# Scaling attention weights before mixing, or mixed values after it: a change in two of four attentions of a two-block transformer kernel

## The chip, the cores and the metric

The kernel runs on one core of one Trainium2 chip. The metric is the device time of one execution in microseconds. The core's engines are TensorE (PE, with its weight loads as PEld), VectorE (DVE), ScalarE (ACT), GpSimd (POOL) and SyncE (SP), which issues most DMAs. Each engine works through its own instructions in order; semaphores tie them together.

## The reference

Two diffusion-transformer blocks run one after the other on 256 latent and 256 context tokens of width 1024, in fp32. The first has feed-forward layers and two mixers, the second two mixers. Each mixer projects, runs an attention beside a recurrent or linear branch, and projects back. What matters here is the attention of the first block's mixers:

```python
# even mixer: 8 query heads, 2 key heads of width 64
def attend(q, k, v):
    s = jnp.einsum('bqhgd,bkhd->bhgqk', q, k).astype(jnp.float32)
    p = jax.nn.softmax(s, axis=-1).astype(v.dtype)
    return jnp.einsum('bhgqk,bkhd->bqhgd', p, v)
# odd mixer: 16 query heads, 4 key heads; window of 128 positions, context keys, and a sink
s_win = jnp.where(valid, s_win, NEG_BIG)
p = softmax_with_sink(jnp.concatenate([s_win, s_ctx], axis=-1))
o = p[..., :span] @ vb + p[..., span:] @ v_c
```

The softmax's division by the row's sum can stand before the product with the values or behind it. The second block has an MLA attention with an mLSTM branch, and a neighbourhood attention with a gated linear one.

## The kernel before

All activations lie transposed in SBUF: a tile has 128 channels on its partitions and 512 tokens along them (`T`; the latent ones are columns `TC` = 256 to 512). Weights stream through a ring in slabs of 128x1024. ScalarE rounds each slab to its high part (L422), VectorE subtracts to get the low part (L427, `split_lo`), and TensorE multiplies high by high, high by low and low by high (L530 to L532; L538 to L541 where both halves stand in one tile).

**An attention** goes over pairs: two heads (a channel tile `t`) and 128 query tokens (`qt`). `attention_pairs` lists 16 pairs for "even", of which 8 see two key tiles and 8 see four, and 16 for "odd", which see three each. The functions `attend_tensor`, `attend_vector` and `attend_scalar` are generators that walk the same iterations `it`, a software pipeline over pairs:

- TensorE: scores of pair `it` (L1538); transposes of the weights of pair `it-2` (L1553), into banks 4 and 5; product with the values of pair `it-3` (L1571), into a bank from `mix_bank`.
- VectorE: `find_max` of pair `it` (for "odd" a mask is added first, L1595; the maximum is L1601, for "odd" followed by small sink terms, L1605 and L1607); `scale_weights` of pair `it-1` (for "odd" the sums are put together, L1616 and L1619; reciprocal L1622 of two sums a token, drain, two scalings of the weights, L1626, then the semaphore `probs_scaled`); for "even" the copy of the mixed values of pair `it-4` (L1641).
- ScalarE: for "odd" the copy of the mixed values of pair `it-4` (L1654, L1657 rounds a finished tile); copy of the transposed weights of pair `it-2` to SBUF (L1664); two exponentials of pair `it` with their sums (L1679).

TensorE may start the transposes of a pair when `probs_scaled` has counted it. Between these steps `keep_streaming` (L469) puts matmuls of ones with no use for their result, 128 columns each, at places from the table `STREAMED_BEFORE_TURNS`. A matmul of fp32 data has two records in the trace.

**Even attention** stands alone between the even projection and the chunked recurrence ("wkv"). Beside its iterations VectorE does some rotary sums (L1772 to L1781) and the decay sums of the recurrence (L2704, L2710, after two of the iterations), ScalarE three decay exponentials (L2556 to L2558), and GpSimd prepares the recurrence's keys (L2637 to L2647). The recurrence starts when the last mixed values are copied (`mixed_copied`).

**Odd attention** runs beside the odd input projection: for each of eight query slabs TensorE does a slab's 24 matmuls, turns the queries for the rotary sum (L1818), and takes two iterations of the attention. VectorE rotates the queries (L1842 to L1848) and splits the next slab. At its end stand the first two slabs of the output projection: `odd_out_half` is called for slab 0 ahead of the last mixing and for slab 1 behind it. `residual_vector` splits both slabs and six, then two more, tiles of the mixer's output (L1245) for them.

**The mLSTM branch** of the second block has 8 units (head and direction). `mlstm_tensor` makes scores for a head (L3125) and sums for each unit (L3140), which wait for `unit_done` of the unit before and for its own weights. `mlstm_vector` weighs unit `u` (L3040), normalises unit `u-1` (L3052 to L3065, with a reciprocal of four numbers, L3057) and masks unit `u+2` (L3030). Ahead of the sums of units 0 and 2 stand ten matmuls of ones.

Of the kernel before, what the change touches and what calls it, by code (L numbers as in the profile page):

```python
# [23 lines left out]
ALU = mybir.AluOpType  # L24
# [3 lines left out]
P = 128  # L28
D = 1024
KT = D // P  # L30
TC = 256
# [229 lines left out]
def build(nc, xin, ctx2, condrows, stream_k, stream_f, vecs, consts, tables, small, nabias, out):  # L261
# [4 lines left out]
    with ExitStack() as ctx:  # L266
# [122 lines left out]
        probs_ready = sem("probs_ready")  # L389
        probs_scaled = sem("probs_scaled")  # L390
        probs_turned = sem("probs_transposed")
# [78 lines left out]

        STREAMED_BEFORE_TURNS = {("even", 0): 4, ("even", 1): 3, ("even", 6): 11, ("odd", 10): 8, ("odd", 14): 7}
        STREAMED_BEFORE_ODD_SLAB = {5: (0, 7), 7: (6, 6)}
# [774 lines left out]
        def residual_vector(dve, r):  # L1247
# [3 lines left out]
            if r == 1:  # L1251
                split_lo(dve, first_place(stage, 0), n0, s0 + 1)
                for kt in range(6):
                    odd_tile_lo(dve, kt)
                split_lo(dve, 1, n0 + 1, s0 + 2)
                for kt in range(6, KT):
                    odd_tile_lo(dve, kt)
# [235 lines left out]
        def attention_turned(which, u):  # L1493

            two = BIG[:, 16 + u % 2 * 2:18 + u % 2 * 2, :] if which == "odd" else WORK[:, 20 + u % 2 * 2:22 + u % 2 * 2, :]
            return two.rearrange("p b t -> p (b t)")

        def mix_bank(which, u):

            return pb[6] if which == "odd" else pb[6 + u % 2]  # L1500

        def attend_tensor(pe, a):
# [12 lines left out]
            for it in range(n + 3):  # L1515
# [25 lines left out]
                if 0 <= u < n:  # L1541
# [4 lines left out]
                    keep_streaming(pe, pb[4], STREAMED_BEFORE_TURNS.get((which, u), 0))  # L1546
                    pe.wait_ge(probs_scaled, u0 + u + 1)
                    nt = len(key_tiles(which, pairs[u][1]))
                    for b in range(2):
                        for i in range(nt):  # L1550
                            o = slice((b * nt + i) * HD, (b * nt + i + 1) * HD)
                            for h, half in enumerate(HALF):
                                mm = pe.transpose(pb[4 + h][:, o], attention_probs(which, u)[half, b, tok(i)], C("ident")[half, half])  # L1553
                    mm.then_inc(probs_turned, 1)
                u = it - 3
                if 0 <= u < n:
# [18 lines left out]
                    if which == "odd" and u == n - 1:  # L1575
                        odd_out_half(pe, 1, range(KT - 1))
                yield

        def attend_vector(dve, a):
# [30 lines left out]
            def scale_weights(u):  # L1610
# [4 lines left out]
                if which == "odd":  # L1615
                    dve.tensor_tensor(st[:, 4, :], st[:, 4, :], st[:, 3, :], ALU.add)  # L1616
                    dve.drain()
                    if pairs[u][1] == 3:
                        dve.scalar_tensor_tensor(out=st[:, 4, :], in0=st[:, 2, :], scalar=C("padkeys"), in1=st[:, 4, :],  # L1619
                                                 op0=ALU.mult, op1=ALU.add)  # L1620
                        dve.drain()
                dve.reciprocal(st[:, 1, :], st[:, 4, :])  # L1622
                dve.drain()
                for b in range(2):
                    probs = attention_probs(which, u)[:, b, 0:nk]
                    ins = dve.tensor_scalar(probs, probs, st[:, 1, b:b + 1], None, ALU.mult)  # L1626
                ins.then_inc(probs_scaled, 1)

            for it in range(n + 4):
                turns_first = which == "odd" and it in (1, 13)  # L1630
                if turns_first:
# [5 lines left out]
                u = it - 4  # L1637
                if 0 <= u < n and which != "odd":
                    t, qt = pairs[u]
# [5 lines left out]
        def attend_scalar(act, a):  # L1645
# [3 lines left out]
            for it in range(n + 4):  # L1649
                u = it - 4  # L1650
                if 0 <= u < n and which == "odd":
                    t, qt = pairs[u]
                    act.wait_ge(mixed, u0 + u + 1)
                    act.activation(BIG[:, t, qt * P:qt * P + P], pb[6][:, 0:P], ACT.Copy).then_inc(mixed_copied, 1)  # L1654
                    if qt == 3:
                        act.drain()
                        act.activation(out_hi(1, t), BIG[:, t, TC:T], ACT.Copy).then_inc(mixer_hi, 1)  # L1657
                u = it - 2
                if 0 <= u < n:
                    nk = len(key_tiles(which, pairs[u][1])) * P  # L1660
                    act.wait_ge(probs_turned, u0 + u + 1)
                    if u >= 2:
                        act.wait_ge(mixed, u0 + u - 1)
                    act.activation(crossed(attention_turned(which, u)[:, 0:2 * nk]),  # L1664
# [1453 lines left out]
        def mlstm_tensor(pe):  # L3118
# [10 lines left out]
            def sums(u):  # L3129
                d, h = UNITS[u]  # L3130
                if u:
                    pe.wait_ge(unit_done, u)
                if u in (0, 2):
                    keep_streaming(pe, pb[6], 10)
# [868 lines left out]
```

## Time and profile before

| | |
|---|---|
| median of 3 runs | 2481.13 us (2480.53 to 2483.14) |
| the profiled execution | 2482.91 us, its span 2481.1 us |
| busy in it | TensorE 96%, VectorE 69%, ScalarE 43%, GpSimd 15% |
| mean granted clock of TensorE | 0.997 of full speed |
| even attention, first scores to last copy | 534.0 to 583.8 us |
| odd attention, first scores to last mixing | 1607.2 to 1678.8 us |
| sums of the mLSTM's units | 2157.3 to 2197.8 us |

A row of an instruction gives start, duration, engine, line, operation, the tiles written and read, their shapes and, in brackets, for how long the engine had stood idle before it and what it waited for. Engines overlap the end of one instruction with the next, so start to next start is somewhat less than the duration. TensorE's ends are modelled.

### The profile page before, as it was taken

To read this page: it belongs to the slowest core of one execution; us is meant where nothing else is said; L and a number is where in the kernel's file an instruction comes from. 1 tells how busy PE (TensorE), PEld (TensorE's weight loads), DVE (VectorE), ACT (ScalarE), POOL (GpSimd) and SP (SyncE) were. 2 spreads that over 40 slices of the span, in tenths; PEclk is the share of its full clock that TensorE was granted. 3 is DMA by queue.
4 is the path that set the end of the run, shared out by engine and by line. 5 is a ranking of instruction groups with operands and counts; after the bars stand their busy time and mean duration, and the time that the engine had idled before them with its cause. 6 is when DMAs were issued, how large, how long until landed. Compare 5 with 4: busy or idle time off the path is not lost.

```text
span 2481.1 us, 46363 instructions
## 1 busy us (share of the span) xinstructions
PE 2393.4 (96%) x17990; PEld 1935.5 (78%) x17990; DVE 1712.5 (69%) x2826; ACT 1062.4 (43%) x1748; POOL 378.7 (15%) x350
## 2 busy tenths in 40 slices
PE   7999999998889999999999999989999999999988
PEld 4888888866776878888788888768888885678866
DVE  3877787667565787778787773687777334776676
ACT  4232224356444622222532222475556334656354
POOL 2000001022444200000100001101002711211052
PEclk9999999999999999999999999999999999999999
DMA  7655664210000265566465553315564223113311
GB/s 291 227 191 192 197 198 129 94 39 3 4 4 20 102 212 194 194 195 200 148 211 194 191 181 97 110 43 167 187 180 136 94 94 91 38 45 128 116 46 52
DMA packets 89017, 324.84 MB, mean 131 GB/s; under 512 B 9888, under 2 KB 11040, under 8 KB 88096
## 3 DMA queue, kind: packets, MB, share of 16 engines
q1 hardware_dynamic: 86768, 310.15, 38.9%
q0 software_dynamic: 2096, 12.55, 1.5%
q8 instruction: 108, 1.77, 0.3%
q14 instruction: 45, 0.37, 0.0%
HBM read 321.49 MB, written 1.18 MB: 130 GB/s over the span
## 4 chain that ended last, share of the span: by engine, by line
PE 82%; DVE 9%; issue 3%; ACT 3%; DVEq 1%; DMA 1%; POOLq 0%; POOL 0%; ACTq 0%; SPq 0%
PE bank L530 20%; PE bank L532 20%; PE bank L531 20%; PE bank L540 5%; PE bank L541 3%; DVE row_statistics L1601 1%; PE bank L1538 1%; DVE weights_hi_lo L427 1%; DVE work L1626 1%; PE bank L1571 1%; DMA projections<-stream_k 1%; PE bank L2441 1%; PE bank L539 1%; PE bank L1994 1%; PE bank L3448 1%
## 5 line engine op out<-in xcount | busy, mean ns | idle before, releaser
L422 ACT ACTIVATE weights_hi_lo<-weight_ring 128x1024 fp32r<-128x1024 f32 (+1 forms) x338 | 352.1, 1042 | 991.4 <-PE bank L532 935.8
L530 PE MATMUL bank<-input_hi,weights_hi_lo 128*128 128x512 f32 (+1 forms) x1688 | 642.0, 380 | 7.3 <-DVE weights_hi_lo L427 4.3
L427 DVE TENSOR_TENSOR weights_hi_lo<-weight_ring,weights_hi_lo 128x1024 fp32r<-128x1024 f32 (+1 forms) x333 | 403.3, 1211 | 351.2 <-ACT weights_hi_lo L422 349.6
L531 PE MATMUL bank<-input_lo,weights_hi_lo 128*128 128x512 f32 (+1 forms) x1688 | 638.1, 378 | 0.0
L532 PE MATMUL bank<-input_hi,weights_hi_lo 128*128 128x512 f32 (+1 forms) x1688 | 638.1, 378 | 0.0
L530 PEld LDWEIGHTS bank<-input_hi,weights_hi_lo 128*128 128x128 f32 x1688 | 317.4, 188 | 75.1 <-issue 9.0
L532 PEld LDWEIGHTS bank<-input_hi,weights_hi_lo 128*128 128x128 f32 x1688 | 317.5, 188 | 59.5
L531 PEld LDWEIGHTS bank<-input_lo,weights_hi_lo 128*128 128x128 f32 x1688 | 317.5, 188 | 59.2 <-issue 0.7
L815 POOL TENSOR_TENSOR work<-work 128x512 f32<-128x512 f32 (+1 forms) x48 | 68.4, 1425 | 1220.2 <-ACT work L700 1219.3
L606 DVE CUSTOM_DVE_ANT_0 work<-weight_ring,extra_tiles 128x1024 f32<-128x1024 f32 x176 | 224.5, 1276 | 35.7 <-issue 13.3
L530 PE MATMUL bank<-hidden_hi_lo,weights_hi_lo 128*128 128x512 f32 x632 | 246.8, 391 | 0.0
L532 PE MATMUL bank<-hidden_hi_lo,weights_hi_lo 128*128 128x512 f32 x632 | 245.9, 389 | 0.0
L531 PE MATMUL bank<-hidden_hi_lo,weights_hi_lo 128*128 128x512 f32 x632 | 245.9, 389 | 0.0
L607 DVE CUSTOM_DVE_ANT_0 weight_ring<-weight_ring,extra_tiles 128x1024 f32<-128x1024 f32 x176 | 214.9, 1221 | 0.0
L531 PEld LDWEIGHTS bank<-hidden_hi_lo,weights_hi_lo 128*128 128x128 f32 x632 | 118.6, 188 | 25.1 <-issue 0.5
L530 PEld LDWEIGHTS bank<-hidden_hi_lo,weights_hi_lo 128*128 128x128 f32 x632 | 118.6, 188 | 25.0 <-ACT work L2807 0.2
L532 PEld LDWEIGHTS bank<-hidden_hi_lo,weights_hi_lo 128*128 128x128 f32 x632 | 118.6, 188 | 24.8
L1601 DVE TENSOR_REDUCE row_statistics<-bank 128x2 f32<-128x1024 f32 (+2 forms) x56 | 55.7, 994 | 25.5 <-PE bank L1538 23.5
L1413 DVE TENSOR_TENSOR work<-work,bank 128x512 f32<-128x512 f32 x66 | 45.4, 688 | 36.9 <-PE bank L532 32.8
L427 DVE TENSOR_TENSOR hidden_hi_lo<-weight_ring,hidden_hi_lo 128x1024 fp32r<-128x1024 f32 (+1 forms) x45 | 53.9, 1198 | 15.0 <-ACT hidden_hi_lo L422 14.7
L726 DVE SCALAR_TENSOR_TENSOR input_lo<-residual_stream,modulation,input_hi 128x256 fp32r<-128x256 f32 x96 | 58.4, 649 | 7.4 <-ACT input_hi L715 3.7
L700 ACT ACTIVATE work<-residual_stream 128x512 f32<-128x512 f32 (+1 forms) x72 | 40.9, 577 | 50.8 <-DVE residual_stream L1134 22.9
(600 smaller groups left out, 3749.1 us busy)
## 6 DMA issues: line engine op xcount, KB each, us to landing
weight_ring<-stream_k SPq DMA_DIRECT2D x481, 512.0 KB, 3.5
weight_ring<-stream_f SPq DMA_DIRECT2D x64, 448.0 KB, 3.5
weight_ring<-stream_f SPq DMA_DIRECT2D x32, 512.0 KB, 3.7
projections<-stream_k SPq DMA_DIRECT2D x14, 512.0 KB, 5.6
extra_tiles<-condrows POOLq DMA_DIRECT2D x3, 1024.0 KB, 7.4
constants<-consts POOLq DMA_DIRECT2D x1, 2112.5 KB, 8.6
residual_stream<-xin SPq DMA_DIRECT2D x1, 2048.0 KB, 9.6
work<-nabias POOLq DMA_DIRECT2D x1, 2048.0 KB, 9.5
```

Of the source, the lines that this page charges most:

```text
L422: act.activation(split_place(place)[:, 0, 0:words], w[:, 0:words], ACT.Copy).then_inc(hi_ready, 1)
L427: eng.tensor_tensor(split_place(place)[:, 1, 0:words], ring[:, n % RING, 0:words], split_place(place)[:, 0, 0:words].bitcast(F32), ALU.sub ...
L530: pe.matmul(out, weights[:, 0, w], x_hi, start=first, stop=False)
L531: pe.matmul(out, weights[:, 0, w], x_lo, start=False, stop=False)
L532: return pe.matmul(out, weights[:, 1, w], x_hi, start=False, stop=last)
L540: pe.matmul(bank[:, :], weights[:, 0, w], x_lo_hi, start=first, stop=False)
L541: return pe.matmul(bank[:, TC:T], weights[:, 1, w], x_lo_hi[:, TC:T], start=False, stop=False)
L606: dve.tensor_tensor_reduce(PRODUCTS, w, COND[:, 0, :], 1.0, 0.0, ALU.mult, ALU.add, MOD_SUMS[:, j, 0:1])
L607: dve.tensor_tensor_reduce(w, w, COND[:, 1, :], 1.0, 0.0, ALU.mult, ALU.add, MOD_SUMS[:, j, 1:2]) .then_inc(mod_read, 1)
L726: ins = dve.scalar_tensor_tensor(out=H_LO[:, kt, p:q], in0=X[:, kt, p:q], scalar=MODS[:, scale + kt, s:s + 1], in1=H_HI[:, kt, p:q].bitcas ...
L815: pool.tensor_tensor(total, total, squares_of(place, kt)[:, a:b], ALU.add)
L1601: ins = dve.tensor_reduce(st[:, 0, :], sc[:, :, 0:nk], AX.X, ALU.max, negate=True)
```

## The change

In the "even" and "odd" attention the exponentials are no longer scaled. `scale_weights` writes reciprocals of the two sums, each spread over 64 columns, as a tile of 128x128, and ends there. TensorE starts the transposes when the exponentials are there (`probs_ready`), then waits for the reciprocals and multiplies them with the identity, so that their tokens come to lie along the free axis and their heads over the partitions: one matmul into the free half of the mixing bank for "even", two of 64 columns behind the transposed weights for "odd". ScalarE copies the result to SBUF, for "even" by an instruction of its own, for "odd" with the transposed weights, whose copy grows from 768 to 896 columns. A new function `normalise` multiplies the mixed values by it on VectorE; it takes the place of VectorE's copy for "even" and of ScalarE's for "odd", and stands at the head of an iteration instead of its end. The last "odd" product stands in `residual_vector`, ahead of the split of the second output slab. Nine matmuls of ones are added ahead of the transposes of even pair 3, and the ten ahead of the sums of mLSTM unit 2 are taken out.

```diff
-        STREAMED_BEFORE_TURNS = {("even", 0): 4, ("even", 1): 3, ("even", 6): 11, ("odd", 10): 8, ("odd", 14): 7}
+        STREAMED_BEFORE_TURNS = {("even", 0): 4, ("even", 1): 3, ("even", 3): 9, ("even", 6): 11, ("odd", 10): 8, ("odd", 14): 7}
...
                 for kt in range(6):
                     odd_tile_lo(dve, kt)
+                normalise(dve, 1, len(attention_pairs("odd")) - 1)
                 split_lo(dve, 1, n0 + 1, s0 + 2)
...
+        NORMALISED_AFTER = ("even", "odd")
+        def reciprocals(which, u):
+            tile = BIG[:, 29, 0:TC] if which == "even" else BIG[:, 24, TC:T]
+            return tile[:, tok(u % 2)]
+        def spread_reciprocals(which, u):
+            if which == "even":
+                return BIG[:, 29, TC:T][:, tok(u % 2)]
+            return attention_turned(which, u)[:, tok(6)]
...
-                    pe.wait_ge(probs_scaled, u0 + u + 1)
+                    pe.wait_ge(probs_ready if which in NORMALISED_AFTER else weights_scaled, u0 + u + 1)
...
+                    if which in NORMALISED_AFTER:
+                        pe.wait_ge(weights_scaled, u0 + u + 1)
+                        if which == "even":
+                            if u >= 2:
+                                pe.wait_ge(mixed_copied, u0 + u - 1)
+                            mm = pe.matmul(mix_bank(which, u)[:, P:TC], reciprocals(which, u), C("ident"), start=True, stop=True)
+                        else:
+                            for h, half in enumerate(HALF):
+                                mm = pe.matmul(pb[4 + h][:, 6 * HD:7 * HD], reciprocals(which, u), C("ident")[:, half],
+                                               start=True, stop=True)
                     mm.then_inc(probs_turned, 1)
...
+        def normalise(dve, a, u):
+            which, u0 = ATTENTIONS[a], pairs_before(a)
+            t, qt = attention_pairs(which)[u]
+            out = BIG[:, t, tok(qt)] if which == "odd" else H[:, t, tok(qt)]
+            dve.wait_ge(mixed, u0 + u + 1)
+            dve.tensor_tensor(out, mix_bank(which, u)[:, 0:P], spread_reciprocals(which, u), ALU.mult).then_inc(mixed_copied, 1)
...
+                if which in NORMALISED_AFTER:
+                    dve.reciprocal(reciprocals(which, u).rearrange("p (b c) -> p b c", b=2), along(st[:, 4, :], HD))\
+                       .then_inc(weights_scaled, 1)
+                    return
...
             for it in range(n + 4):
+                if it >= 4 and which in NORMALISED_AFTER and (which, it) != ("odd", n + 3):
+                    normalise(dve, a, it - 4)
...
-                if 0 <= u < n and which != "odd":
+                if 0 <= u < n and which not in NORMALISED_AFTER:
...
                     t, qt = pairs[u]
-                    act.wait_ge(mixed, u0 + u + 1)
-                    act.activation(BIG[:, t, qt * P:qt * P + P], pb[6][:, 0:P], ACT.Copy).then_inc(mixed_copied, 1)
                     if qt == 3:
-                        act.drain()
+                        act.wait_ge(mixed_copied, u0 + u + 1)
...
                     if u >= 2:
-                        act.wait_ge(mixed, u0 + u - 1)
+                        act.wait_ge(mixed_copied if which == "odd" else mixed, u0 + u - 1)
+                    if which == "even":
+                        act.activation(spread_reciprocals(which, u), mix_bank(which, u)[:, P:TC], ACT.Copy)
+                    else:
+                        nk += HD if which == "odd" else 0
...
-                if u in (0, 2):
+                if u == 0:
                     keep_streaming(pe, pb[6], 10)
```

## Rows read from the trace of the kernel before

**Rows 1.** The page: the span, and the chain that ended last by engine.

```profile
span 2481.1 us, 46363 instructions
...
PE 82%; DVE 9%; issue 3%; ACT 3%; DVEq 1%; DMA 1%; POOLq 0%; POOL 0%; ACTq 0%; SPq 0%
```

**Rows 2.** Table by stretches: length, busy time of each engine, clock, DMA.

```profile
558.90:583.90 25.00, 21.83 (x303) 14.73 (x302) 20.09 (x49) 19.12 (x45) 5.24 (x5) 1.00 0.01 2
...
551.00:552.00 1.00, 1.00 (x15) 0.88 (x14) 0.92 (x3) 1.00 (x3) 0.00 (x0) 0.50 0.00 0
...
1624.78:1633.36 8.58, 7.96 (x83) 6.12 (x84) 7.67 (x22) 6.36 (x18) 0.00 (x0) 1.00 0.22 64
...
2168.00:2171.00 3.00, 3.00 (x17) 3.00 (x17) 2.68 (x6) 1.89 (x6) 2.15 (x2) 0.53 0.43 142
```

**Rows 3.** VectorE in order of time, even attention, two and four key tiles.

```profile
562.83 0.62 DVE L1626 TENSOR_SCALAR work<-work,row_statistics 128x256 f32<-128x256 f32 x2
563.36 0.29 DVE L1641 COPY mixer_io<-bank 128x128 f32<-128x128 f32 x1
...
574.89 0.16 DVE L1622 RECIPROCAL row_statistics<-row_statistics 128x2 f32<-128x2 f32 x1
575.12 0.88 DVE L1626 TENSOR_SCALAR work<-work,row_statistics 128x512 f32<-128x512 f32 x2
575.92 0.28 DVE L1641 COPY mixer_io<-bank 128x128 f32<-128x128 f32 x1
```

**Rows 4.** VectorE in order of time, odd attention.

```profile
1630.78 0.17 DVE L1622 RECIPROCAL row_statistics<-row_statistics 128x2 f32<-128x2 f32 x1
1631.02 0.75 DVE L1626 TENSOR_SCALAR projections<-projections,row_statistics 128x384 f32<-128x384 f32 x2
1631.69 0.42 DVE L1842 SCALAR_TENSOR_TENSOR projections<-projections,constants 128x256 f32<-128x256 f32 x1
```

**Rows 5.** Order of time, odd attention: one idle time of TensorE and one of VectorE.

```profile
1631.92 0.59 PE L1553 MATMUL bank<-constants,projections 64*128 64x64 f32 x12 [0.62 <-DVE projections L1626]
...
1654.75 0.43 DVE L1595 TENSOR_TENSOR bank<-bank,projections 128x256 f32<-128x256 f32 x1 [1.04 <-PE bank L1538]
```

**Rows 6.** TensorE in order of time, mLSTM, ahead of unit 2.

```profile
2167.51 4.07 PE L469 MATMUL bank<-vectors 128*128 128x128 f32 x20 [1.95 <-DVE work L3065]
2171.37 2.50 PE L3140 MATMUL bank<-projections,work 128*128 128x129 f32 x20
```

**Rows 7.** Groups by shape: count, busy us, mean ns; mLSTM, then odd attention.

```profile
L3057 DVE RECIPROCAL mlstm_denominators<-mlstm_denominators 128x4 f32<-128x4 f32 x8 | 1.4, 178 | 0.6
L3055 DVE TENSOR_TENSOR mlstm_denominators<-bank,mlstm_denominators 128x4 f32<-128x4 f32 x8 | 1.3, 163 | 0.6
...
L1622 DVE RECIPROCAL row_statistics<-row_statistics 128x2 f32<-128x2 f32 x4 | 0.7, 166 | 0.3
```

**Rows 8.** GpSimd and VectorE in order of time, even pairs 6 and 10.

```profile
555.19 1.27 POOL L2641 TENSOR_TENSOR work<-work 128x512 f32<-128x512 f32 x1
...
555.57 2.58 DVE L1626 TENSOR_SCALAR work<-work,row_statistics 128x512 f32<-128x512 f32 x2
...
567.44 1.64 DVE L1626 TENSOR_SCALAR work<-work,row_statistics 128x256 f32<-128x256 f32 x2
```

**Rows 9.** TensorE in order of time: ones ahead of even pair 6.

```profile
556.23 2.72 PE L469 MATMUL bank<-vectors 128*128 128x128 f32 x22
```

**Rows 10.** Order of time at the end of the odd attention.

```profile
1676.88 1.22 DVE L427 TENSOR_TENSOR weights_hi_lo<-weight_ring,weights_hi_lo 128x1024 fp32r<-128x1024 f32 x1
...
1677.96 0.88 PE L1571 MATMUL bank<-projections 128*64 128x128 f32 x12
...
1678.77 0.50 PE L540 MATMUL bank<-hidden_hi_lo,weights_hi_lo 128*128 128x512 f32 x1
```

**Rows 11.** Waits in the odd stage, 1612 to 1684 us: sum, times, longest.

```profile
PE bank L1553 <- DVE projections L1626: 4.0, 5, 0.9
...
PE bank L1571 <- ACT projections L1654: 2.6, 2, 1.9
```

More of the change, by code:

```diff
@@ L389, in build @@
         probs_ready = sem("probs_ready")
-        probs_scaled = sem("probs_scaled")
+        weights_scaled = sem("weights_scaled_or_reciprocals_ready")
         probs_turned = sem("probs_transposed")
@@ L1626, in scale_weights @@
                     ins = dve.tensor_scalar(probs, probs, st[:, 1, b:b + 1], None, ALU.mult)
-                ins.then_inc(probs_scaled, 1)
+                ins.then_inc(weights_scaled, 1)
             for it in range(n + 4):
+                if it >= 4 and which in NORMALISED_AFTER and (which, it) != ("odd", n + 3):
+                    normalise(dve, a, it - 4)
                 turns_first = which == "odd" and it in (1, 13)
```

## The prediction

> **What bounds the kernel now.** I read the page first: the chain that ended last is 82% TensorE and 9% VectorE [rows 1], so work moved off VectorE pays only where VectorE stands in that chain. The change touches three stretches, so I took each in the table by stretches and then in the order of time.
>
> Even attention runs from 534 to 583.9 us. In its second half TensorE is busy 21.8 of 25 us and VectorE 20.1 [rows 2]; no engine is full, and the chain goes from one to the other. VectorE's turn for a pair with four key tiles is: maximum, reciprocal, two scalings of the weights, copy of an older pair's mixed values; of which, from start to next start, the reciprocal with its drain takes 0.23 us (574.89 to 575.12) and the scalings 0.80 (to 575.92). With two key tiles the scalings take 0.53 (562.83 to 563.36) [rows 3].
>
> Odd attention runs beside the odd input projection. A period of two pairs and one slab takes 8.58 us: TensorE is busy 7.96, VectorE 7.67 [rows 2]. The rest of VectorE's time is no idleness but the drains between dependent small instructions: its rows follow each other with no idle time in brackets [rows 4], and TensorE waits 0.62 us before a pair's transposes for the scaling [rows 5]. So here VectorE sets the pace, and every 0.1 us added to its turn is paid by the kernel.
>
> The mLSTM stretch: before its third sum (unit 2) TensorE waits 1.95 us, streams ten matmuls of ones for 3.86 us (start to start), then starts the sum [rows 6]. After that wait the granted clock is 0.53 from 2168 to 2171 us [rows 2], about the lower of TensorE's two levels, 1.2 GHz.
>
> **The price that decides.** Removed in each of the 32 pairs: two scalings and a drain. Added: one VectorE reciprocal that writes 128 elements a partition (two sums, each spread over 64) where the old one wrote 2. No row shows a wide one. The reciprocal of 4 elements takes 178 ns, that of 2 takes 166 in the odd stage, 156 and less in the even [rows 3, 7]; so 6 to 11 ns for an element. A product of 4 elements takes 163 and a copy of 128 takes 0.28 us in all [rows 3, 7], about 1 ns for an element. From 156 ns and the middle of the slopes, 8.4 ns, I estimate 0.156 + 126 x 0.0084 = 1.21 us, 1.13 from start to next start (rows here overlap by 0.08). The bounds: below, as cheap as the copy (0.28, start to start 0.21); above, by 11 ns 1.54 (1.46). I take 1.13, since two shapes of one operation differ by ten times what another operation's elements cost.
>
 By the first the wide reciprocal lies near my middle value and the change costs time; by the second it is the cheap one of the first rival below. The slope in the rows agrees with the first.
>
> **Even attention.** VectorE: reciprocal and scaling go from 1.03 to 1.13 in 8 pairs and from 0.76 to 1.13 in 8: +3.8 us. The product with the spread reciprocals costs what the copy did (0.20 to 0.21). Two scalings of the old kernel lasted 2.58 and 1.64 us (should be 0.88 and 0.62) beside GpSimd's two-input products [rows 8]: 2.7 us that fall away with the scalings, since the new instructions have one SBUF input at most. Net +1.1 on VectorE. The Trainium skill's page "SBUF — State Buffer", section "Who interferes with whom", says the same: such a scaling takes the port pair that GpSimd uses, and the second to issue blocks; by that rule the 2.7 us go entirely.
>
> TensorE gets a 128-column fp32 matmul a pair: 0.25 us, as one of the ones (22 records, two to a matmul, thus 11, in 2.72 [rows 9]); between 0.12 (were it one record) and 0.5 (half clock). ScalarE gets a copy of 128x128: 0.2, priced as VectorE's copy of that shape. I follow the order up to the transposes of pair 6, which now begin at 558.9. Ahead of them the pairs 0 to 5 cost VectorE 4 x 0.37 + 2 x 0.10 = 1.7 more, matmul and copy of pair 5 another 0.5, and about 1.0 comes back: now TensorE idles before pair 4's transposes and the clock then halves for about 3 us (0.50 in 551 to 552 [rows 2]), which costs some 1.5 us of work at half speed, of which VectorE's own work covers 0.5; the nine new ones fill that place. They cost nothing themselves: VectorE's decay sums, 1.9 us in the same place, hide them; without that cover they cost up to 2.2. So +1.2 up to pair 6.
>
> From there to the end of the stretch TensorE is busy 21.8 of 25.0 us now [rows 2], and ten spreading matmuls add 2.5: 24.3. Of the 3.2 us of waits now, those for the scaling go, since the transposes start without it. I keep 2.0: the loop of transposes, spreading and ScalarE's two copies (0.7 where ScalarE's decays stand between, 0.4 twice and 0.5 in the last pairs, which have no other work of TensorE beside them). That makes 26.3, or +1.3. Even attention: **+2.5 us**.
>
> **Odd attention.** VectorE: reciprocal plus scalings take 0.91 from start to start (1630.78 to 1631.69) [rows 4]; they become 1.13: +0.22. ScalarE's copy of the mixed values becomes VectorE's product: +0.21. So +0.43 a pair, for 15.5 pairs +6.7. From that goes what VectorE idles now: 1.04 us at 1654.75 behind the last slab's scores [rows 5], and about 0.8 in the last pairs, whose transposes stand behind ones and mixing. That (1.9 in all) leaves +4.9. TensorE's two 64-column matmuls (0.25 a pair) fit into its waits of 0.6 to 0.9; ScalarE's longer copy (+0.13) against the lost one (-0.2) is even. At the end the last product is put ahead of the split of the second output slab: today that split starts at 1676.88 and is done before TensorE needs it at 1678.77, right after the last mixing [rows 10]. Behind the product it starts 0.3 us after that mixing's end, ends at about 1680.3, and TensorE, busy without a gap from 1675.7, stands 1.5 us. TensorE bounds the output projection, so nothing gives that back. Odd attention: **+6.4 us**.
>
> **mLSTM.** Without the ten ones the sum begins at 2167.5. The clock falls at about 2168.4 in either case, since the wait ahead of it stays, so the half-clock time now falls on the sum: ones and sum need 2.4 + 2.4 at full clock and lost 1.5; alone the sum ends 2.4 earlier. Its weights are ready (VectorE weighs unit 2 before it normalises unit 1). Between 0 (clock low for longer) and 3.9: **-2.5 us**.
>
> **Sum.** +2.5 + 6.4 - 2.5 = +6.4 us on a span of 2481.1; the execution took 2482.9, 1.8 more than the median of the runs, 2481.13. Against the median: 2487.5.
>
> **Rivals.** (1) The wide reciprocal is cheap: VectorE saves 0.91 - 0.21 (reciprocal) - 0.21 (product) = 0.49 a pair in the odd stage and ceases to be its bound. TensorE's waits there, 4.0 for the scalings and 2.6 for ScalarE's mixed copies [rows 11], go; 16 x 0.25 = 4.0 of spreading comes and the late split costs 1.5: -1.1. In the even stage TensorE and ScalarE are full anyhow: +1.5 (the new ones no longer hidden). With -2.5 the sum is -2.1: 2479.0, not slower. Against it: the slope of the rows; for it, that only two widths carry that slope. (The second of the two pages of the Trainium skill named above would make it this case.) It decides from a wide reciprocal under 0.5 us. Chance 0.2, and a third of it goes below -5 us, if early transposes help more than I counted. (2) The upper slope: 1.46 a reciprocal, thus 0.33 more for each of 32 pairs, 10.6, of which I let 2.8 lie beside TensorE's full stretch in the even stage: +14, 2495. Chance 0.12. (3) The reciprocal at 6 ns (0.92 us, 0.84 from start to start): even +1.7, odd 15.5 x 0.14 less the same 1.9 of idle, plus 1.5: +1.8, thus +1.0, 2482. Chance 0.13. (4) A full TensorE pipeline without the half-clock stretches gives back more than the additions cost, about -6, 2475: for it speaks that no transpose waits for a scaling any longer; against it that in the odd stage VectorE is bound whatever TensorE does. Chance 0.05. My forecast holds the remaining 0.5; by itself it reaches from 2483 to 2492.
>
> **Numbers.** A measurement tells this kernel from no change beyond about 0.2%, 5 us: slower above 2486.1, faster below 2476.2. The forecast gives 0.37 slower and 0.13 same, (2) 0.12 slower, (3) 0.13 same, (1) 0.13 same and 0.07 faster, (4) 0.05 faster: 0.12 faster, 0.39 same, 0.49 slower. The range leaves out the far part of (2) and (4): 2477 to 2494.
>
> **What would show it.** The reciprocal of 128x128: 1.2 us, not 0.3 nor 1.5. Odd period 9.4 instead of 8.58 with VectorE without idle. No instruction of 2.58 us at even pair 6. Clock 1.0 through the even stage. A gap of 1.5 us in TensorE before the second odd output slab. Sum 2 of the mLSTM right at the end of unit 1's products, half clock over it, everything later 2.5 us closer. Wrong would make me: a wide reciprocal at copy speed, or a TensorE wait in the odd period that isn't VectorE's.

## The result and the profile after

The changed kernel takes 2495.1 us (median of 6 runs, 2493.91 to 2499.18) against 2481.71 (6 runs) of the kernel before: ratio 1.0058, 95% interval 1.0048 to 1.0068. That is slower, as forecast, but by twice as much (13.4 us instead of 6.4): 2487.5 was said, and 2495.1 lies 1.1 us above the range of 2477 to 2494. The profiled execution took 2494.22 us; its span is 11.3 us longer, so 2 us of the medians' difference are not in the traces. The page:

```profile
span 2492.4 us, 46477 instructions
...
PE 83%; DVE 8%; ACT 4%; issue 3%; DMA 1%; DVEq 1%; POOLq 0%; POOL 0%; ACTq 0%; SPq 0%
```

The chain says nearly what it said before [rows 1]: it can't tell where 11 us came in. So I laid the two traces side by side by TensorE's matmuls (the same line, its first or its last instruction) and read how much later each starts. The differences between these marks are the table on which all the rest stands. Its columns are the stretches; the rows below the first are the experiments, told further down. The first 530 us are left out: they scatter by 3.6 us from kernel to kernel, with the same work in them. "All three" are the order at the end, the cheap reciprocal and the spreading by transposes; "tiny matmuls" move the code behind them and do nothing else.

| later or earlier than in the kernel before, us | even att. 534-583 | recurrence 583-790 | to 1599 | odd loop to last transposes 1675 | odd end to 1679 | to 2157 | mLSTM to end |
|---|---|---|---|---|---|---|---|
| the change | +2.6 | +2.6 | +0.3 | +3.8 | +5.5 | -0.4 | -2.8 |
| even alone | +2.6 | +3.9 | +0.2 | +0.3 | +0.1 | -0.3 | -1.2 |
| odd alone | -0.8 | +0.6 | -0.1 | +4.2 | +5.7 | -0.3 | +0.4 |
| ones of unit 2 out, alone | -0.8 | -1.2 | -0.1 | +0.4 | 0.0 | +0.2 | -2.8 |
| change, order at the end mended | +2.6 | +2.6 | +0.3 | +5.4 | +0.6 | -0.3 | -2.8 |
| change, two reciprocals and a copy | +2.6 | +1.9 | 0.0 | +2.0 | +4.1 | -0.3 | -2.2 |
| change, transposes spread | +1.0 | +3.8 | +0.3 | +2.4 | +5.1 | -0.4 | -2.8 |
| change, all three | +0.5 | +3.1 | 0.0 | +0.3 | +0.1 | -0.3 | -2.8 |
| before, 25 tiny matmuls at its start | -0.8 | +1.9 | -0.1 | +2.1 | 0.0 | -0.1 | 0.0 |
| before, 70 of them | 0.0 | -1.8 | -0.1 | +2.0 | 0.0 | +0.2 | 0.0 |
| odd with all three, ones out | 0.0 | +1.8 | 0.0 | -0.3 | 0.0 | -0.1 | -2.9 |
| even alone, 40 tiny matmuls | +2.6 | +1.0 | +0.2 | +0.3 | 0.0 | -0.1 | -1.3 |

Each row is one execution, and the table has to be read with its own scatter. Ahead of the end of the recurrence, four of these kernels have the same program: the one before, odd alone, ones out alone, and odd with all three, ones out. Their recurrences are 0, +0.6, -1.2 and +1.8. A part of the scatter is the clock: stretches of a few microseconds at 0.5 of full speed (1.2 GHz) stand in some traces and not in others at the same place. Of the six kernels with the even attention as before, the one before and two more have such a stretch at about 551 us [rows 2]; the three rows with -0.8 have none. So a difference of 0.8 us in the first column can be the clock alone, and one of 1.4 to 2.1 in the odd stage and the mLSTM (below); and one of 3 us in the recurrence is no sign of an edit by itself.

**The wide reciprocal.** Groups of VectorE by shape, the changed kernel:

```profile
L1655 DVE RECIPROCAL projections<-row_statistics 128x128 f32<-128x128 f32 x32 | 30.4, 948 | 3.8 <-ACT work L1719 2.6
...
L1658 DVE RECIPROCAL row_statistics<-row_statistics 128x2 f32<-128x2 f32 x24 | 3.8, 156 | 0.8 <-ACT work L1719 0.6
```

(948 - 156) / 126 is 6.3 ns an element: the lower of my two slopes [rows 7], not their middle. A copy of that shape takes about 0.28 us [rows 3].

**The even stage.** By stretches (length, busy time of each engine, clock, DMA):

```profile
558.90:583.90 25.00, 23.88 (x306) 17.52 (x306) 18.60 (x28) 19.80 (x55) 5.67 (x6) 1.00 0.01 2
...
551.00:552.00 1.00, 1.00 (x22) 0.81 (x18) 0.82 (x1) 1.00 (x3) 0.00 (x0) 1.00 0.00 0
```

Against [rows 2] TensorE is busy 2.05 us longer in the same 25, VectorE 1.5 less, and the half-clock stretch is gone. None of the seven kernels with the nine ones has it, but neither have three of six without them; against those three the even stage costs 3.4 us, not 2.6. TensorE's share of it, in order of time:

```profile
548.60 0.46 PE L1567 MATMUL bank<-constants,work 64*128 64x64 f32 x8
548.99 0.49 PE L1573 MATMUL bank<-constants,projections 128*128 128x128 f32 x2
549.41 0.66 PE L1595 MATMUL bank<-work,projections 128*64 128x128 f32 x8
```

The spreading matmul holds TensorE 0.42 us from its start to the next one's, not the 0.25 of a matmul of ones in a row of its like. VectorE beside GpSimd's products:

```profile
555.62 0.95 DVE L1655 RECIPROCAL projections<-row_statistics 128x128 f32<-128x128 f32 x1 [0.66 <-ACT work L1719]
556.49 1.88 DVE L2744 TENSOR_TENSOR_SCAN projections<-spare_tiles,projections 128x512 f32<-128x512 f32 x1
558.45 1.53 DVE L2750 TENSOR_TENSOR projections<-projections 128x512 f32<-128x512 f32 x1
```

GpSimd's product beside them took longer as well, 2.18 us where it took 1.45 before:

```profile
557.25 2.18 POOL L2687 TENSOR_TENSOR work<-projections,work 128x512 f32<-128x512 f32 x1
```

The stall of 2.58 us is gone [rows 8], but the decay sums came to lie in its place. The kernel before had them just behind GpSimd's work:

```profile
558.28 1.21 DVE L2704 TENSOR_TENSOR_SCAN projections<-spare_tiles,projections 128x512 f32<-128x512 f32 x1
559.56 0.69 DVE L2710 TENSOR_TENSOR projections<-projections 128x512 f32<-128x512 f32 x1
```

So 1.5 us of the 1.7 won there were lost again. The Trainium skill ("SBUF — State Buffer", section "Who interferes with whom") says that a VectorE instruction with two SBUF inputs contends with a GpSimd one that reads SBUF; both of these have two, and the trace agrees with 1.88 against 1.21 and 1.53 against 0.69 us.

**The odd stage.** By stretches, one period of two pairs and a slab, 1641.90 - 1632.60 = 9.30 us; then VectorE in order of time; then TensorE:

```profile
1632.30:1641.60 9.30, 8.96 (x93) 7.23 (x92) 8.10 (x20) 6.15 (x16) 0.00 (x0) 1.00 0.19 58
```

```profile
1641.03 0.95 DVE L1655 RECIPROCAL projections<-row_statistics 128x128 f32<-128x128 f32 x1
1641.90 1.16 DVE L427 TENSOR_TENSOR weights_hi_lo<-weight_ring,weights_hi_lo 128x1024 fp32r<-128x1024 f32 x1
1642.98 0.28 DVE L1609 TENSOR_TENSOR projections<-bank,projections 128x128 f32<-128x128 f32 x1
1643.72 0.43 DVE L1627 TENSOR_TENSOR bank<-bank,projections 128x256 f32<-128x256 f32 x1 [0.46 <-PE bank L1552]
```

```profile
1638.89 0.88 PE L1595 MATMUL bank<-projections 128*64 128x128 f32 x12 [0.34 <-DVE projections L1609]
...
1681.62 0.66 PE L1576 MATMUL bank<-constants,projections 128*128 128x64 f32 x4
1682.21 0.88 PE L1595 MATMUL bank<-projections 128*64 128x128 f32 x12
```

The period is the 9.4 that I said, but not for my reason. TensorE is busy 8.96 of 9.30 (7.96 of 8.58 before [rows 2]); the two spreading matmuls (four records) take 0.59 us a pair. VectorE stands idle 0.46 in each period, waiting for scores, and a mixing waits 0.34 us for the product that empties its bank.

**The end of the odd attention**, VectorE, then TensorE:

```profile
1683.14 0.29 DVE L1609 TENSOR_TENSOR projections<-bank,projections 128x128 f32<-128x128 f32 x1 [1.00 <-PE bank L1595]
1685.32 0.29 DVE L1609 TENSOR_TENSOR projections<-bank,projections 128x128 f32<-128x128 f32 x1 [1.89 <-PE bank L1595]
1685.53 1.22 DVE L427 TENSOR_TENSOR first_weights_hi_lo<-weight_ring,first_weights_hi_lo 128x1024 fp32r<-128x1024 f32 x1
...
1691.76 0.29 DVE L1609 TENSOR_TENSOR projections<-bank,projections 128x128 f32<-128x128 f32 x1 [3.00 <-PE bank L1595]
1691.96 1.21 DVE L427 TENSOR_TENSOR weights_hi_lo<-weight_ring,weights_hi_lo 128x1024 fp32r<-128x1024 f32 x1
```

```profile
1687.23 0.76 PE L540 MATMUL bank<-hidden_hi_lo,first_weights_hi_lo 128*128 128x512 f32 x1 [1.95 <-DVE hidden_hi_lo L1245]
...
1693.23 0.50 PE L540 MATMUL bank<-hidden_hi_lo,weights_hi_lo 128*128 128x512 f32 x1 [1.52 <-DVE weights_hi_lo L427]
```

VectorE's last three products stand waiting 5.89 us for mixings, and both splits of the output projection are queued behind them. TensorE waits twice: 1.95 us for the first slab and its tiles, which I had not seen, and the 1.52 for the second that I had (1.5). Behind the first wait the clock fell as well, by stretches:

```profile
1687.00:1690.50 3.50, 3.27 (x11) 2.88 (x12) 1.75 (x6) 0.00 (x0) 0.00 (x0) 0.55 0.50 150
```

So the 5.5 us are 3.5 of waits, about 1.4 of half clock (the kernel with two reciprocals and a copy has both waits and no such stretch, and loses 4.1) and 0.6 that stay when the order is mended.

**The mLSTM**, TensorE:

```profile
2177.32 2.40 PE L3180 MATMUL bank<-projections,work 128*128 128x129 f32 x20
2181.67 2.50 PE L3180 MATMUL bank<-projections,work 128*128 128x129 f32 x20 [1.95 <-DVE work L3105]
2184.90 2.85 PE L3165 MATMUL bank<-projections 128*128 128x512 f32 x8 [0.73 <-DVE work L3080]
```

The same wait of 1.95 us [rows 6], and no half clock behind it: the sum takes 2.50. In its place stands a wait of 0.73 for the weighing of the next unit. But the clock differs here without the edit too. The same place in even alone, which has the ones, and then in the changed kernel with two reciprocals and a copy, which has not:

```profile
2172.76 2.50 PE L469 MATMUL bank<-vectors 128*128 128x128 f32 x20 [1.95 <-DVE work L3104]
```

```profile
2177.53 4.14 PE L3182 MATMUL bank<-projections,work 128*128 128x129 f32 x20 [1.95 <-DVE work L3107]
```

With the ones and at full clock: -1.2 against the kernel before. Without them, the sum at half clock: -2.2. Without them and at full clock: -2.8. The ones are worth 1.6 at full clock and 2.2 where the half clock falls in both kernels.

### The profile page after: what moved, and what is told of

Same layout as the page of the kernel before. It is cut to its first block, busy times and chain, and to the rows that moved or that the text cites. A ratio compares the mean times of both kernels' runs of the same rounds, so it can differ in the third digit from the quotient of the medians.

```text
span 2492.4 us, 46477 instructions
## 1 busy us (share of the span) xinstructions
PE 2406.3 (97%) x18084; PEld 1947.7 (78%) x18084; DVE 1714.4 (69%) x2778; ACT 1062.6 (43%) x1748; POOL 379.8 (15%) x350
## 4 chain that ended last, share of the span: by engine, by line
PE 83%; DVE 8%; ACT 4%; issue 3%; DMA 1%; DVEq 1%; POOLq 0%; POOL 0%; ACTq 0%; SPq 0%
PE bank L530 20%; PE bank L532 20%; PE bank L531 20%; PE bank L540 5%; PE bank L541 3%; PE bank L1552 1%; PE bank L1595 1%; DVE row_statistics L1633 1%; DVE weights_hi_lo L427 1%; DMA projections<-stream_k 1%; PE bank L539 1%; PE bank L2481 1%; PE bank L2034 1%; PE bank L1567 1%; PE bank L3488 1%
```

## The experiments

**Each part alone.** Even alone: the even edit with its nine ones, odd attention and mLSTM as before. The main line of it (the rest puts the other parts back):

```diff
-NORMALISED_AFTER = ("even", "odd")
+NORMALISED_AFTER = ("even",)
```

> Only the even attention is changed, with its nine ones; odd attention and mLSTM are as before. The traces of before and after say +2.5 us inside the even stage and, by the account that TensorE's stalls without a cause in the recurrence are a matter of where its longer instruction stream lies (fetching), another +2.6 between 620 and 790 us: +5 in all, 2487. Rival: those 2.6 us are an accident of one execution or come from the odd or mLSTM edit; then +2.5, 2484.

2490.0 us against 2482.01, ratio 1.0040 (1.0026 to 1.0054). Odd alone, the same with `("odd",)`:

> Only the odd attention is changed; even attention and mLSTM are as before. By the traces +9.1 us (3.8 to the last transposes, 5.3 at the end of the stage): 2490.8. My prediction had 6.4 with a dearer reciprocal, thus 3.5 with the measured one: 2485. Nothing may move between 534 and 1600 us.

2492.35, ratio 1.0047 (1.0030 to 1.0065). The ones alone: the kernel before with `if u == 0` in place of `if u in (0, 2)`.

> The kernel before without the ten matmuls of ones ahead of mLSTM unit 2. Theory: TensorE's sum starts 3.9 us earlier and runs at half clock for a while: -2.5 to -2.9 us, 2479. Rival: the ones only filled a wait, or the clock stays low for longer: 0.

2478.8, ratio 0.9990 (0.9981 to 1.0000). In the table the parts add up to the whole within 0.6: even +2.6, odd +9.9 (9.3 in the whole), mLSTM -2.8. What is left is the recurrence, which no edit touches and in which even alone lost 3.9 us.

**The order at the end.** The changed kernel with the first split behind the last reciprocal, the six tiles an iteration later, the second split ahead of the last product:

```diff
-                split_lo(dve, first_place(stage, 0), n0, s0 + 1)
-                for kt in range(6):
-                    odd_tile_lo(dve, kt)
-                normalise(dve, 1, len(attention_pairs("odd")) - 1)
                 split_lo(dve, 1, n0 + 1, s0 + 2)
+                normalise(dve, 1, len(attention_pairs("odd")) - 1)
...
+                if which == "odd" and it == n:
+                    split_lo(dve, first_place("odd_out", 0), SLAB_AT["odd_out"][0], SPLIT_AT["odd_out"][0] + 1)
+                if which == "odd" and it == n + 1:
+                    for kt in range(6):
+                        odd_tile_lo(dve, kt)
```

> The changed kernel, but VectorE splits the first slab of the odd output projection right behind the last reciprocals, the six tiles one iteration later, and the second slab ahead of the last product. Theory: VectorE's waits for the mixing of pairs 13 to 15 stood ahead of work that TensorE needs, and the +5.3 us at the end of the stage are those; 4 to 5 us come back: 2490.5 against 2495.1. Rival: only the last product's place matters (my prediction): 1.5 come back. Rival: the mixing itself is late by the spreading: nothing comes back.

2490.28, ratio 1.0040 (1.0026 to 1.0054). VectorE, then TensorE of this kernel:

```profile
1680.55 0.95 DVE L1652 RECIPROCAL projections<-row_statistics 128x128 f32<-128x128 f32 x1
1681.42 1.16 DVE L427 TENSOR_TENSOR first_weights_hi_lo<-weight_ring,first_weights_hi_lo 128x1024 fp32r<-128x1024 f32 x1
1684.04 0.29 DVE L1606 TENSOR_TENSOR projections<-bank,projections 128x128 f32<-128x128 f32 x1 [1.47 <-PE bank L1592]
```

```profile
1678.70 3.06 PE L469 MATMUL bank<-vectors 128*128 128x128 f32 x14 [0.54 <-ACT projections L1706]
...
1686.11 0.50 PE L540 MATMUL bank<-hidden_hi_lo,first_weights_hi_lo 128*128 128x512 f32 x1
...
1689.23 0.50 PE L540 MATMUL bank<-hidden_hi_lo,weights_hi_lo 128*128 128x512 f32 x1
```

The split lies in VectorE's idle time, TensorE reaches both slabs without a wait, and the end costs 0.6 instead of 5.5 us. The loop lost 1.6 more: the seven matmuls of ones took 3.06 us here, 1.83 in the changed kernel, since the half clock came here and not at the end, by stretches:

```profile
1679.00:1682.50 3.50, 3.50 (x26) 3.19 (x25) 3.20 (x6) 1.93 (x5) 0.00 (x0) 0.51 0.00 0
```

Loop and end together gave back 3.3 us, about the two waits (3.47): the queue's order was their cause. The other 1.6 of the end only moved.

**The reciprocal.** The changed kernel with the reciprocal of two sums as before, and a copy to 128 columns:

```diff
-                    dve.reciprocal(reciprocals(which, u).rearrange("p (b c) -> p b c", b=2), along(st[:, 4, :], HD))\
+                    dve.reciprocal(st[:, 1, :], st[:, 4, :])
+                    dve.drain()
+                    dve.tensor_copy(reciprocals(which, u).rearrange("p (b c) -> p b c", b=2), along(st[:, 1, :], HD))\
                        .then_inc(weights_scaled, 1)
```

> The changed kernel, but the reciprocal is taken of the two sums as before and then copied out to 128 columns: 0.23 + 0.20 = 0.43 us of VectorE a pair instead of 0.87. Theory: TensorE, not VectorE, sets the odd period of 9.32 us now (VectorE waits 0.46 us in it for scores), and TensorE with ScalarE the even stage, so this gives back 1 us at most, 2494. Rival (the step of my prediction): VectorE is the bound, 0.44 for each of 31 pairs: -8 to -13 us, 2484.

2492.14, ratio 1.0043 (1.0027 to 1.0060). Its copy, by groups:

```profile
L1657 DVE COPY projections<-row_statistics 128x128 f32<-128x128 f32 x32 | 8.1, 254 | 2.3
```

In the odd stage 3.2 us came back: 1.8 in the loop, more than the 1 us at most that I expected, and 1.4 at the end, which is the half clock that didn't come here (both waits did):

```profile
1684.00:1688.00 4.00, 3.13 (x24) 2.46 (x24) 2.36 (x8) 0.08 (x1) 0.00 (x0) 1.00 0.36 131
```

In the even stage nothing came back: beside the spreading matmuls the reciprocal was not on the path.

**The spreading matmuls.** The changed kernel with transposes:

```diff
-mm = pe.matmul(mix_bank(which, u)[:, P:TC], reciprocals(which, u), C("ident"), start=True, stop=True)
+mm = pe.transpose(mix_bank(which, u)[:, P:TC], reciprocals(which, u), C("ident"))
...
-mm = pe.matmul(pb[4 + h][:, 6 * HD:7 * HD], reciprocals(which, u), C("ident")[:, half], start=True, stop=True)
+mm = pe.transpose(pb[4 + h][:, 6 * HD:7 * HD], reciprocals(which, u)[half, :], C("ident")[half, half])
```

> The changed kernel, but TensorE spreads the reciprocals by transposes (one record each) instead of fp32 matmuls with the identity (two records and two weight loads each, 0.42 us from start to start for even, 0.59 for odd). Theory: the matmuls are what makes TensorE the bound; their price falls to 0.1 to 0.2, -3 us in even and -3 in odd (there VectorE bounds again, at 8.9 us a period): 2489. Rival: a wait that TensorE has beside them takes their place: 0.

2491.38, ratio 1.0039 (1.0025 to 1.0054). TensorE of this kernel, even stage:

```profile
546.38 0.33 PE L1573 MATMUL bank<-constants,projections 128*128 128x128 f32 x1
546.64 0.66 PE L1594 MATMUL bank<-work,projections 128*64 128x128 f32 x8
```

0.26 us instead of 0.42, one record instead of two. The even stage's cost falls from 2.6 to 1.0, the odd loop's from 3.8 to 2.4, about half of the 3 us each that I expected.

**All three** in one kernel:

> The changed kernel with all three: order at the end of the odd stage, reciprocal of two with a copy, spreading by transposes. Theory: both engines are relieved, the odd period comes near TensorE's 8.4 us: 2495.1 - 4.8 (order) - 6 (spreading) - 3 to 5 (reciprocal, now that TensorE no longer hides it): 2480. Rival: the gains overlap, 2486.

2484.19 (10 runs), ratio 1.0014 (1.0004 to 1.0023). TensorE, then VectorE of this kernel:

```profile
1634.50 0.88 PE L1591 MATMUL bank<-projections 128*64 128x128 f32 x12 [0.97 <-DVE projections L1605]
...
1643.38 0.88 PE L1591 MATMUL bank<-projections 128*64 128x128 f32 x12 [0.96 <-DVE projections L1605]
```

```profile
1638.16 0.28 DVE L1605 TENSOR_TENSOR projections<-bank,projections 128x128 f32<-128x128 f32 x1
1639.33 0.43 DVE L1623 TENSOR_TENSOR bank<-bank,projections 128x256 f32<-128x256 f32 x1 [0.89 <-PE bank L1549]
```

The even stage costs 0.5, the odd one 0.4; the whole came out 4 us above what I expected, for the gains overlap. And the odd period is still 8.88 us with no engine full. With both prices gone, the wait that the change brings shows plainly: the mixed values have one bank, the product that empties it stands on VectorE behind the rotary sums, so a mixing waits 0.97 us for VectorE, and VectorE 0.89 us for the scores behind that mixing.

**The place of the code.** The kernel before with 25 matmuls of one column ahead of its first work:

```diff
+for _ in range(25):
+    pe.matmul(pb[7][0:1, 0:1], V("ones", 0, 1), V("ones", 0, 1), start=True, stop=True)
 first_mods_tensor(pe)
```

> The kernel before with 25 fp32 matmuls of one column at its start, where TensorE waits for the first weights: 50 records, as many as the even edit adds. They only move the code behind them. Theory: TensorE's stalls without a cause in the recurrence (seven or eight of 0.6 to 1.5 us) lie at other instructions then, and that stage's length changes by 1 to 4 us, in the sum +2.5, 2484.5. Rival: the stalls and the stage stay as in the kernel before: 0, 2482.

2484.87 (10 runs), ratio 1.0013 (1.0003 to 1.0023). Waits of TensorE in the recurrence for which the trace shows no releaser, kernel before, then this one:

```profile
626.64 0.21 PE L2527 MATMUL bank<-spare_tiles,extra_tiles 64*64 64x64 f32 x1 [0.80 <-issue]
...
629.99 0.73 PE L2362 MATMUL bank<-work 64*64 64x64 f32 x33 [1.26 <-issue]
```

```profile
623.82 0.76 PE L2512 MATMUL bank<-extra_tiles,spare_tiles 64*64 64x128 f32 x18 [0.91 <-issue]
...
627.55 0.27 PE L2521 MATMUL bank<-extra_tiles,spare_tiles 64*64 64x64 f32 x2 [1.35 <-issue]
```

They came earlier in the same work, but at the same place in the list: counted from the start of the trace, these two waits stand ahead of TensorE's matmul records 4204 and 4332 in both kernels, though 25 such matmuls put 50 records ahead. The two are 128 records apart (each with a weight load), and so are other pairs of such waits. All thirteen traces bear this out: twelve have a wait of 0.9 to 1.8 us at record 4326 to 4332, whatever work stands there, and the kernel with 70 has it at 4460, 128 further on. So such a wait keeps its place in the list of TensorE's instructions, not in the work. And the end of the odd attention, by stretches, kernel before, then this one:

```profile
1667.00:1670.00 3.00, 2.28 (x29) 1.41 (x29) 2.54 (x8) 2.92 (x9) 0.00 (x0) 1.00 0.00 0
1670.00:1673.00 3.00, 2.77 (x30) 2.41 (x32) 2.06 (x10) 3.00 (x8) 0.00 (x0) 1.00 0.03 5
```

```profile
1667.00:1670.00 3.00, 2.63 (x30) 1.68 (x30) 2.33 (x8) 2.92 (x9) 0.00 (x0) 0.70 0.00 0
1670.00:1673.00 3.00, 3.00 (x19) 2.67 (x20) 2.19 (x11) 3.00 (x9) 0.00 (x0) 0.50 0.00 0
```

The same work behind the same wait of 1.94 us, and once the clock halves, once it doesn't: 2.1 us. (The kernel with 70 has this half clock too, behind the same wait.) Two more kernels ask whether this holds with another count, and whether the even edit leaves something behind in the recurrence. The kernel before with 70:

> The kernel before with 70 one-column matmuls ahead of its first work instead of 25, nothing else. Theory (waits of TensorE with no releaser, and the stretches at half clock that follow when one lies near a wait, hang on the place of the code and not on its work): the recurrence from 583 to 790 us, which took 1.9 longer with 25, takes some other time, between 1.5 shorter and 3 longer, with the waits at other instructions; and the odd attention's end either loses the 2.1 us that it lost with 25, or doesn't. Rival (25 were just late by chance of the run, the code's place does nothing): recurrence within 0.3 of before and no wait moved.

2482.63 (10 runs), ratio 1.0007 (0.9997 to 1.0016). The recurrence is 1.8 shorter; its waits of over half a microsecond, nine for 8.4 us before (one listed twice, so eight for 7.1), are three for 3.9. Even alone with 40:

> The even edit alone again (odd and mLSTM as before), with 40 one-column matmuls ahead of the kernel's first work. There the even stage lost 2.5 us and the recurrence 3.9. Theory (the recurrence's loss is a matter of the code's place): the even stage again +2.5, the recurrence something between 0 and 4, and its waits without a releaser at other instructions than at 626, 630, 676, 726, 730, 771 and 775 us. Rival (the even edit itself leaves something behind that slows the recurrence): again 3.5 to 4.3 longer. The median then is about 2490 minus what the recurrence gives back.

2487.21 (10 runs), ratio 1.0019 (1.0009 to 1.0028). Even stage again +2.6; the recurrence's loss 1.0 instead of 3.9. The places of the waits are shown by this, their length and the recurrence's is not: +1.9, -1.8 and the 2.9 between the two kernels with the even edit all lie within the 3.0 by which four kernels with the same program differ there. In the seven kernels with the even edit the recurrence is +1.0 to +3.9, in the six without it -1.8 to +1.9. So the even edit does seem to cost something there, by the code's place or by what it leaves behind; these runs don't separate the two.

**The best of the parts**: odd with all three mends, the even attention as before, the ones out.

> The odd attention of the changed kernel with the three mends (the splits ahead of the last products, reciprocal of two sums with a copy, transposes in place of the two matmuls), the even attention as in the kernel before, no ones ahead of mLSTM unit 2. In the kernel with all three the odd stage came out 0.4 us longer than before and the mLSTM 2.8 shorter; the recurrence behind an untouched even attention was 0.6 longer with the odd edit and 1.2 shorter with none. Theory: 2.4 us less than before in all, with the recurrence's scatter of about 1 on it: 2479 us, ratio 0.999. Rival (the gain of the mends hangs on the even stage too, since only there transposes are early in a full TensorE): as before or slower, 2482 to 2485.

2479.3 (11 runs), ratio 0.9992 (0.9983 to 1.0001). By the table it gains 0.3 in the odd loop and 2.9 in the mLSTM and loses 1.8 in the recurrence; that is no gain that these runs can tell from none, and taking the ones out alone does as much.

## Why the prediction was off, point by point

- **Even attention, +2.5: 2.6.** The parts were less right than the sum, so the match is in part luck. Up to pair 6 I said +1.2; its ones start at 557.02 instead of 556.23 [rows 9], 1.1 with the start's 0.3. The reciprocal, my chief cost, counted for nothing (a cheap one left the +2.6 as it was; with transposes it gave 0.5); the matmul, 0.42 us and not 0.25, carried 1.6 of it. Of "2.7 us that fall away with the scalings", 1.5 came back in the decay sums.
- **Odd loop, +4.9: 3.8.** The price of the reciprocal was too high (1.13 from start to start, measured 0.87), and the step that TensorE's spreading "fit into its waits of 0.6 to 0.9" failed: 0.59 a pair filled them. Two errors of opposite sign. Making either cheap brought back 1.4 to 1.8, both with the mended order 3.5, so neither engine alone was the bound.
- **Odd end, +1.5: 5.5. This is the step that broke the forecast.** I followed the one product that the diff moves and priced its wait rightly (1.5, measured 1.52). I took it as given that TensorE finds the first slab split, and did not ask what the other products do: in the last iterations no maximum is left between them, so the products of pairs 13 and 14, now at an iteration's head on VectorE, wait for their mixings in the queue ahead of the first split. Before, ScalarE did those waits. The split of slab 0 starts 11.8 us later than it did (1673.7, now 1685.5), and TensorE stands 1.95 us for it. Mending the order removed both waits. A further 1.4 us is the half clock behind the first wait, which the sum had at nothing; it came in three of the four kernels with this order, so it is partly chance.
- **mLSTM, -2.5: -2.8.** Near, by another path: I let the half clock fall on the sum "since the wait ahead of it stays"; the wait stayed and the clock was 1.00. A new wait of 0.7 for the weighing took part of the gain. The path that I described came in one kernel, with two reciprocals and a copy: sum at half clock, no new wait, -2.2. Whether the clock halves there is not the ones' doing as far as these runs tell: it did in four of six kernels with them and in one of seven without.
- **Not foreseen: the recurrence, +2.6.** The sum had nothing for it, and why it is longer stays open. Where TensorE stops without a releaser depends on how many of its instructions stand ahead; for how long it stops differs even with the same program (7.1, 5.4, 5.8 and 6.4 us in waits of over half a microsecond in the four kernels with the same one). The changed kernel has 8.5, and the clock fell to 0.60 in 778 to 782 us, where the kernel before had 1.00 (last fence below). That the two waits just ahead (1.54 and 1.22 us, then 1.98 for VectorE) made it fall isn't shown: with 25 tiny matmuls waits of 1.25 and 1.24 stood ahead of one of 1.99 and it stayed at 1.00. What stops the engine the trace doesn't show; that its code has to be fetched is my guess. The Trainium skill ("Runtime: NRT & Kernel Launch", section "Instruction fetch mechanics") has fetching mostly hidden as long as no branch is taken; if that is so, the waits are something else, and no run here tells the two apart.
- **Rivals.** (3), the reciprocal at 6 ns, came true in its price and not in its 2482, since it shared my step on the odd end and my matmul. (2) named 2495 by a reciprocal of 1.54 us, which it isn't. (1) would have needed under 0.5 us; with exactly that (0.17 and 0.25) the kernel took 2492.14, so even the cheap case was not a gain. Nothing of (4) showed: the half-clock stretch at 551 us went, and the additions still cost more than it gave back. That the measured 2495.1 is the figure of (2) is chance.
- The signs that I listed: odd period 9.4 (9.30), no 2.58 us (none), clock 1.0 in the even stage, the gap of 1.5 ahead of slab 1: right. Reciprocal 1.2 us, "VectorE without idle", half clock over sum 2: wrong.

The clock in the changed kernel's recurrence, by stretches:

```profile
778.00:782.00 4.00, 3.31 (x4) 1.08 (x4) 0.96 (x3) 1.95 (x3) 0.63 (x1) 0.60 0.00 0
```

## What to carry to other kernels

Who waits matters as much as who works: when an instruction moves to another engine, list what that engine has queued behind it, above all in the last iterations, where nothing is left to fill the wait. Price a lone fp32 matmul from the nearest lone one and not from a row of its like, and ask if a transpose does the same. And lay two traces side by side by common marks before explaining a difference, but take the scatter of each stretch from kernels whose program is the same up to its end: here that was 3 us in 200, as much as the difference to be explained. A copy of the old kernel with idle instructions ahead shows whether waits hang on the code's place.

## What the runs showed of the hardware

- The reciprocal costs 6.3 ns an element (156 ns for 2, 948 for 128). "VectorE: DVE Perf Modes" of the Trainium skill (section "First, the fixed hardware budget") has it repeat, and the trace agrees in that it is several times a copy's price.
- The same 128x128 fp32 tile through TensorE: matmul with the identity 0.42 us, two records; transpose 0.26, one.
- TensorE's waits without a releaser of 0.5 to 1.8 us stay at the same count of its matmul records (4204, 4332) when 25 matmuls are put 600 us ahead of them, and pairs of them lie 128 records apart.
- Behind the same wait of 1.94 us the clock stayed at 2.4 GHz in three of the six kernels with the odd attention as before and fell to 1.2 in the other three (0.4 us lost in one, 2.0 to 2.1 in two), with nothing changed near it. Behind the mLSTM's wait of 1.95 it fell in five of thirteen.
